# Moving the weight buffers of a split-precision kernel: high parts first, 128 spare bytes, then the raw slots

## The chip, the cores and the metric

One core of a Trainium2 chip runs the whole program. The time is the device time of one execution in microseconds. Weights come from the chip's memory through DMA queues; TensorE (PE, with its weight loads as PEld) multiplies, VectorE (DVE), ScalarE (ACT) and GpSimd (POOL) do the rest.

## What is computed

Two blocks in a row on 256 tokens of width 2048, all in float32. The first has two layers: an attention layer (two kinds of heads, 256 context tokens beside the 256 of the sequence, gates, a post-norm with modulation) and a Fourier layer (a two-dimensional FFT over tokens and channels in 16 groups, between two wide projections). The second has a mixer (a gated delta rule in both directions, and attention in three dilations) and a feed-forward part with a depthwise convolution. Most of the arithmetic lies in products of 256 activations with large weight matrices:

```python
z = h @ w_in                                               # attention, 2048 x 4928
u, gate = jnp.split(h @ w_in, 2, axis=-1)                  # Fourier, 2048 x 8192
proj = jnp.einsum("bsd,dp->bsp", n, w_in)                  # second mixer
up = depthwise_conv_centered(jnp.einsum("bsd,df->bsf", n, w_ffn_in), conv_ffn_w)
...
return jnp.einsum("bsf,fd->bsd", jax.nn.silu(gate) * val, w_ffn_out)
```

## The kernel before

**Units.** The host packs all weights into 479 units, in the order in which they are needed. A unit is up to 2048 floats per partition (8 KiB on each of 128 partitions): a few 128-row slices of a matrix by up to 768 columns. `UNITS` lists them; a `Linear` (`("ff", 3)`, `("oX", 1, 0)`, `"ckv"` and so on) is one product's share of them. 447 of the 479 are "split"; the others are `ada` units of the head, which are used as they land.

**Split precision.** A split unit goes through four hands. SP's queue loads it into a raw slot (L718). ACT copies it, rounded, into a high buffer as fp32r (L1459, in `act_hi`). DVE subtracts the high part from the raw weights and writes the remainder, the low part, back over the same raw slot (L2156, in `dve_lo`). PE then runs three matmuls for each slice and output tile (`pe_unit`; all matmuls are issued by the helper at L727): high weights by high activations, high weights by low activations, low weights by high activations. In most products the weights are the stationary operand and the 256 tokens move; in `fu`, `dv` and a few others the activations are stationary and the weights move.

**Buffers and their turns.** One tensor `slab` of 53,132 floats per partition holds all that lives in SBUF, and regions of it are laid out by hand. Region `W`, at offset 0, holds four raw slots and three high buffers of 2048 floats each (L518 to L520), and 32 floats (128 bytes) more, which nothing uses. Region `K` follows (constants, activations `X`), then `R` (everything that changes from stage to stage, such as the activations `H` and their high and low parts). In the head, the first 44 units, two more raw slots and one more high buffer exist inside `R`: by the code's sizes `high[3]` begins 4800 bytes past a multiple of 8192 bytes from the slab's start, `raw[4]` likewise, and `raw[5]` 7712 bytes past one. All seven buffers of `W` begin at exact multiples of 8192 bytes from the slab's start. `RAW_OF` and `HIGH_OF` give each unit its buffers by number: six and four in turn in the head, then four and three in turn.

**Order.** Each engine runs its own program and waits on semaphores. SP's DMA for a unit waits until PE has used the unit that held the raw slot before; ACT's copy waits for the landing and for the high buffer to come free; DVE's subtraction waits for ACT; PE waits for DVE. ACT and DVE run two units ahead of PE (`act_hi(LIN[name].us[n] + 2)`). The norms, softmaxes, the delta rule and the Fourier steps run as side work between units. In the delta rule four work areas, `gL`, `gY`, `gG[0]` and (through `gL`) `rhs[0]`, are laid over `high[0]`, `high[1]` and `high[2]` (L660 to L661), while no unit needs them.

The lines that matter: 

```python
W = Region(0, UNIT * (SLOTS + HIGH) + 32)                  # L518
raw = [W.place(UNIT) for _ in range(SLOTS)]
high = [W.place(UNIT) for _ in range(HIGH)]
K = Region(W.size, KEEP)
R = Region(W.size + KEEP, SLAB - KEEP - W.size)
```

Of the kernel before, what the change touches and what calls it, by code (L numbers as in the profile page):

```python
# [19 lines left out]
UNIT = 2048  # L20
SLOTS = 4
HIGH = 3
# [423 lines left out]
def program(nc, a, out, cmaps):  # L446
    with ExitStack() as ctx:
# [68 lines left out]
                return named  # L516

        W = Region(0, UNIT * (SLOTS + HIGH) + 32)  # L518
        raw = [W.place(UNIT) for _ in range(SLOTS)]
        high = [W.place(UNIT) for _ in range(HIGH)]  # L520
        K = Region(W.size, KEEP)
        R = Region(W.size + KEEP, SLAB - KEEP - W.size)

# [2620 lines left out]
```

## Time and profile before

| what | us |
|---|---|
| median of 3 runs | 2887.72 |
| lowest, highest | 2879.97, 2899.77 |
| the profiled execution | 2913.37 |
| span of the profiled execution, first to last instruction | 2911.6 |
| PE matmul busy | 2786.7 |
| DVE busy | 1809.9 |
| ACT busy | 1246.7 |

The profiled execution is longer than each of the three timed runs. The span is cut into stages by the order of the units: the head (0 to about 160 us), attention (to about 700), the Fourier layer (to about 1290), dilated attention (to about 1727), the delta rule (to about 2072), and from there the output product and the feed-forward part up to the end.

### The profile page before, as it was taken

What the parts mean: (1) busy time and instruction counts of PE and PEld (TensorE: products, weight loads), DVE (VectorE), ACT (ScalarE), POOL (GpSimd) and SP (SyncE); (2) the same over time, 40 slices, a digit from 0 to 9 for tenths busy, and PEclk for the clock granted to TensorE, in tenths of its full rate; (3) what the DMA queues carried; (4) which work ended last, traced back from release to release, by engine and by line L of the source; (5) the groups of instructions that cost most, each with busy time, mean ns of one, the idle gap of its engine ahead of it and who ended that gap; (6) DMA issues with size and microseconds to landing.
All of it is one profiled execution on the core that took longest, in us unless ns stands there. A gap on an engine that the chain in (4) does not pass through costs nothing.

```text
span 2911.6 us, 50366 instructions
## 1 busy us (share of the span) xinstructions
PE 2786.7 (96%) x22070; PEld 2638.8 (91%) x22070; DVE 1809.9 (62%) x2229; ACT 1246.7 (43%) x1375; POOL 270.2 (9%) x330
## 2 busy tenths in 40 slices
PE   6899999998999999989999999989999999999998
PEld 3598877797988998989999999979999999999998
DVE  2358767688777545566556555795666665466653
ACT  4323444345443334444434448453544443344444
POOL 0022002120111000003113110021000000000000
PEclk9899999998999999999999999999999999999999
DMA  9867535574776554435555544430445555555553
GB/s 368 325 226 247 194 133 201 202 277 149 251 247 225 192 199 162 169 136 190 174 173 175 174 167 146 154 139 1 145 160 188 189 181 188 189 184 187 183 185 138
DMA packets 93034, 546.84 MB, mean 188 GB/s; under 512 B 12656, under 2 KB 12816, under 8 KB 47888
## 3 DMA queue, kind: packets, MB, share of 16 engines
q1 hardware_dynamic: 69552, 466.39, 45.3%
q0 software_dynamic: 20480, 67.13, 6.8%
q10 hardware_dynamic: 2784, 10.11, 0.9%
q8 instruction: 174, 2.85, 0.4%
q14 instruction: 44, 0.36, 0.0%
HBM read 541.48 MB, written 2.10 MB: 187 GB/s over the span
## 4 chain that ended last, share of the span: by engine, by line
PE 67%; DVE 6%; ACT 2%; issue 2%; DMA 1%; DVEq 0%; ACTq 0%
PE bank L727 67%; DVE r L2156 2%; DVE f L2727 1%; ACT r L1459 1%; PE bank L787 1%; DVE f L2193 0%; DMA f<-in_later 0%; DVE f L2791 0%; ACT f L1821 0%; DVE f L2788 0%; DVE f L2804 0%; DVE f L2780 0%; DVE f L2539 0%; DMA f<-in_units 0%; DVE f L2556 0%
## 5 line engine op out<-in xcount | busy, mean ns | idle before, releaser
L727 PE MATMUL bank<-r,r 128*128 128x256 f32 (+1 forms) x19596 | 2444.1, 287 | 44.8 <-DVE r L2156 20.5
L727 PEld LDWEIGHTS bank<-r,r 128*128 128x128 f32 x19596 | 2376.2, 190 | 100.8 <-DVE r L2156 28.2
L2156 DVE TENSOR_TENSOR r<-f,r 128x2048 fp32r<-128x2048 f32 (+2 forms) x447 | 961.1, 2151 | 724.4 <-ACT r L1459 723.1
L1459 ACT CAST r<-f 128x2048 fp32r<-128x2048 f32 (+2 forms) x447 | 792.7, 1775 | 886.4 <-PE bank L727 684.2
L727 PE MATMUL bank<-f,f 128*128 128x128 f32 (+10 forms) x1992 | 326.5, 375 | 58.2 <-DMA f<-in_units 23.1
L727 PEld LDWEIGHTS bank<-f,f 128*128 128x128 f32 (+3 forms) x1992 | 218.8, 177 | 121.7 <-issue 53.1
L2193 DVE SCALAR_TENSOR_TENSOR f<-f,f,f 128x512 f32<-128x512 f32 x240 | 179.8, 749 | 53.8 <-DMA f<-in_later 38.2
L3052 POOL DMA_DIRECT2D f<-in_later x256 | 137.5, 537 | 799.8 <-DVE f L2193 475.8
L2727 DVE SCALAR_TENSOR_TENSOR f<-f,f,f 128x255 f32<-128x255 f32 (+1 forms) x272 | 132.9, 491 | 8.8
L1476 ACT COPY f<-bank 128x512 f32<-128x512 f32 x149 | 83.9, 584 | 115.6 <-PE bank L727 109.3
L3061 POOL TENSOR_TENSOR f<-f,f 32x512 f32<-32x512 f32 x24 | 62.7, 2614 | 658.4 <-DVE f L2665 658.4
L787 PEld LDWEIGHTS bank<-f,f 128*128 128x128 f32 x416 | 48.6, 146 | 41.5 <-issue 18.6
L787 PE MATMUL bank<-f,f 128*128 128x128 f32 x416 | 62.7, 284 | 13.7 <-ACT f L1642 9.2
L1642 ACT ACTIVATE f<-bank,f 128x512 f32<-128x512 f32 x32 | 22.0, 688 | 94.8 <-DVE f L2394 86.5
L3064 POOL TENSOR_TENSOR f<-f,f 32x512 f32<-32x512 f32 x24 | 43.7, 1820 | 1.9
L1776 ACT ACTIVATE f<-f,f 128x512 f32<-128x512 f32 x16 | 11.6, 724 | 75.1 <-DVE f L2684 75.1
L2392 DVE TENSOR_REDUCE f<-bank 128x1 f32<-128x512 f32 x32 | 22.0, 689 | 26.3 <-PE bank L727 26.3
L2199 DVE TENSOR_TENSOR f<-bank,f 128x8 f32<-128x8 f32 x8 | 1.3, 166 | 57.0 <-PE bank L727 57.0
L1592 ACT ACTIVATE f<-f 128x256 f32<-128x256 f32 (+1 forms) x46 | 17.3, 430 | 41.4 <-PE bank L727 41.3
L1752 ACT COPY f<-bank 128x254 f32<-128x254 f32 x16 | 5.9, 372 | 66.1 <-PE bank L727 66.1
L2718 DVE TENSOR_SCALAR f<-f,f 128x256 f32<-128x256 f32 x88 | 30.6, 347 | 0.0
L2416 DVE TENSOR_TENSOR f<-bank,f 128x512 f32<-128x512 f32 x24 | 16.6, 692 | 18.7 <-PE bank L727 17.7
(235 smaller groups left out, 925.2 us busy)
## 6 DMA issues: line engine op xcount, KB each, us to landing
f<-in_units SPq DMA_DIRECT2D x346, 1024.0 KB, 4.8
f<-in_units SPq DMA_DIRECT2D x124, 768.0 KB, 4.3
f<-in_later POOLq DMA_DIRECT2D x256, 256.0 KB, 4.3
f<-in_units SPq DMA_DIRECT2D x8, 576.0 KB, 4.4
f<-in_x ACTq DMA_DIRECT2D x2, 1024.0 KB, 12.8
f<-in_ctx ACTq DMA_DIRECT2D x2, 1024.0 KB, 12.2
f<-in_x_turned ACTq DMA_DIRECT2D x1, 2048.0 KB, 13.4
out<-f SPq DMA_DIRECT2D x4, 256.0 KB, 3.7
```

What stands on the lines that cost most here:

```text
L727: return e.matmul(o, lhsT, rhs, start=start, stop=stop, skip_group_check=True)
L787: ins = e.transpose(o[:, j * 128:(j + 1) * 128], src(j), ident)
L1459: e.copy(unit_view(high[HIGH_OF[u]][1], u), unit_view(raw[RAW_OF[u]][0], u)).then_inc(*up("w_hi", ("hi", u)))
L1476: return e.copy(dst, src(ps("lin", name, q))).then_inc(*up("act_out", ("out", "lin", name, q), *names))
L1642: e.activation(probs[i // 16][0][:, i % 3, :], ps("sc", i)[:, :], ACT.Exp, bias=mx[:, 1, i:i + 1], scale=scale, accum_out=mx[:, 2, i:i + 1 ...
L2156: e.tensor_tensor(unit_view(raw[RAW_OF[u]][1], u), unit_view(raw[RAW_OF[u]][0], u), unit_view(high[HIGH_OF[u]][1], u).bitcast(F32), ALU.su ...
L2193: ins = e.scalar_tensor_tensor(o, w, s, o, ALU.mult, ALU.add)
L2718: ins = e.tensor_scalar(o, s, tap(r), None, ALU.mult) if width == 3 else None
L2727: ins = e.scalar_tensor_tensor(o[:, lo:hi], s[:, lo + d:hi + d], tap(j), o[:, lo:hi], ALU.mult, ALU.add)
L3052: e.dma_start(own[:, m % 4, :], a["later"][m // 16, m // 2 % 8, :, m % 2 * 512:m % 2 * 512 + 512]).then_inc(*up(f"own_quarter{m % 4}", ("o ...
L3061: e.tensor_tensor(v, v, cos2.unsqueeze(1).to_broadcast([32, 2, T]), ALU.mult).then_inc(*up("pool_dil"))
L3064: e.tensor_tensor(v, v, two(rt[n % 2][0:32, :]), ALU.add).then_inc(*up("pool_dil", ("roped half", x, hf, br), ("half", n)))
```

## The change

Inside region `W` the three high buffers are placed first, then 32 floats are skipped, then the four raw slots are placed. The region's size is the same, so `K` and `R` and all in them stay where they were. In floats from the slab's start:

| buffer | before | after |
|---|---|---|
| high 0, 1, 2 | 8192, 10240, 12288 | 0, 2048, 4096 |
| raw 0, 1, 2, 3 | 0, 2048, 4096, 6144 | 6176, 8224, 10272, 12320 |
| spare 32 floats | 14336 | 6144 |

```diff
         W = Region(0, UNIT * (SLOTS + HIGH) + 32)
+        high = [W.place(UNIT) for _ in range(HIGH)]
+        W.at += 32
         raw = [W.place(UNIT) for _ in range(SLOTS)]
-        high = [W.place(UNIT) for _ in range(HIGH)]
```

## Rows read from the trace of the kernel before

**Rows 1.** The page: busy time, share of the span, instructions.
```profile
PE 2786.7 (96%) x22070; PEld 2638.8 (91%) x22070; DVE 1809.9 (62%) x2229; ACT 1246.7 (43%) x1375; POOL 270.2 (9%) x330
```
**Rows 2.** The page: the chain that ended last, by engine.
```profile
PE 67%; DVE 6%; ACT 2%; issue 2%; DMA 1%; DVEq 0%; ACTq 0%
```
**Rows 3.** Groups by line and form: busy us, mean ns, idle before and releasers.
```profile
L727 PE MATMUL bank<-r,r 128*128 128x256 f32 x18648 | 2230.9, 282 | 35.9 <-DVE r L2156 20.5 <-issue 8.0 <-DVE r L2592 5.0
L2156 DVE TENSOR_TENSOR r<-f,r 128x2048 fp32r<-128x2048 f32 x314 | 718.7, 2290 | 540.2 <-ACT r L1459 539.9
L1459 ACT CAST r<-f 128x2048 fp32r<-128x2048 f32 x314 | 599.6, 1911 | 672.5 <-PE bank L727 599.6 <-DMA f<-in_units 72.8
...
L1459 ACT CAST r<-f 128x1536 fp32r<-128x1536 f32 x124 | 183.4, 1481 | 210.0 <-DMA f<-in_units 127.9 <-PE bank L727 82.0
```
**Rows 4.** Stretches, L727 alone: from:to, length, PE busy (count), clock, DMA share, GB/s.
```profile
703.00:789.00 86.00, 86.00 (x732) 1.00 0.64 222
922.00:1074.00 152.00, 151.81 (x1339) 1.00 0.58 201
1466.00:1494.00 28.00, 28.00 (x233) 1.00 0.46 157
...
2520.00:2780.00 260.00, 260.00 (x2210) 1.00 0.53 186
```
**Rows 5.** L727 in the stretch 922 to 1074: durations, ns min/median/max.
```profile
L727 PE MATMUL bank<-r,r x1339: 275/276/364, 921.8 to 1073.9; 128*128 128x256 f32 x192
L727 PEld LDWEIGHTS bank<-r,r x1339: 187/188/192, 921.8 to 1073.9; 128*128 128x128 f32 x192
```
**Rows 6.** L727 in the stretch 2520 to 2780: durations, ns min/median/max.
```profile
L727 PE MATMUL bank<-r,r x2210: 280/281/282, 2519.8 to 2780.0; 128*128 128x256 f32 x185
L727 PEld LDWEIGHTS bank<-r,r x2209: 187/188/193, 2519.9 to 2780.0; 128*128 128x128 f32 x185
```
**Rows 7.** L727 on fp32r operands, five stretches from 250 to 2887 us: durations as before.
```profile
L727 PE MATMUL bank<-r,r x669: 273/276/684, 249.7 to 339.9; 128*128 128x256 f32 x166, 40*128 40x256 f32 x2
...
L727 PE MATMUL bank<-r,r x2063: 275/276/476, 891.7 to 1194.2; 128*128 128x256 f32 x153, 128*128 128x512 f32 x35
...
L727 PE MATMUL bank<-r,r x1155: 275/276/582, 1201.5 to 1354.9; 128*128 128x256 f32 x193
...
L727 PE MATMUL bank<-r,r x321: 275/276/369, 1424.8 to 1462.9; 128*128 128x256 f32 x161
...
L727 PE MATMUL bank<-r,r x6816: 280/281/550, 2072.4 to 2886.1; 128*128 128x256 f32 x195
```
**Rows 8.** L2156 and L1459 from 2100 to 2890 us, then 20 to 150; L2156 whole.
```profile
L2156 DVE TENSOR_TENSOR r<-f,r x141: 1751/2292/2294, 2102.9 to 2884.2; 128x2048 fp32r<-128x2048 f32 x125, 128x1536 fp32r<-128x1536 f32 x16
...
L1459 ACT CAST r<-f x141: 1457/1909/1916, 2101.0 to 2882.2; 128x2048 fp32r<-128x2048 f32 x125, 128x1536 fp32r<-128x1536 f32 x16
...
L2156 DVE TENSOR_TENSOR r<-f,r x12: 1748/1759/2293, 47.0 to 147.7; 128x1536 fp32r<-128x1536 f32 x8, 128x2048 fp32r<-128x2048 f32 x4
...
L1459 ACT CAST r<-f x13: 1457/1475/1913, 45.5 to 148.8; 128x1536 fp32r<-128x1536 f32 x8, 128x2048 fp32r<-128x2048 f32 x5
...
L2156 DVE TENSOR_TENSOR r<-f,r x447: 691/2291/2830, 47.0 to 2884.2; 128x2048 fp32r<-128x2048 f32 x100, 128x1536 fp32r<-128x1536 f32 x45, 128x1152 fp32r<-128x1152 f32 x4
```
**Rows 9.** ACT in order of time, 2200 to 2230: start us, us, instruction, idle before.
```profile
2205.58 1.91 ACT L1459 CAST r<-f 128x2048 fp32r<-128x2048 f32 x1 [3.22 <-PE bank L727]
2211.23 1.91 ACT L1459 CAST r<-f 128x2048 fp32r<-128x2048 f32 x1 [3.75 <-PE bank L727]
```
**Rows 10.** The DMA issues of L718, 2100 to 2890 us, then 20 to 150: microseconds to landing.
```profile
DMA to landing us min/median/max: 4.1/4.8/6.7
...
DMA to landing us min/median/max: 4.3/9.3/19.2
```
**Rows 11.** Waits, whole span: who waited for whom, us, times, longest.
```profile
PE bank L727 <- DMA f<-in_units: 23.1, 11, 4.7
PE bank L727 <- DVE r L2156: 20.5, 15, 5.2
```
**Rows 12.** The chain that ended last, shares by line, and its longest piece.
```profile
by line: PE bank L727 66.9%; issue 1.7%; DVE r L2156 1.5%; DVE f L2727 0.6%; ACT r L1459 0.6%; PE bank L787 0.5%; DVE f L2193 0.4%; DMA f<-in_later 0.4%; DVE f L2791 0.4%; ACT f L1821 0.4%; DVE f L2788 0.4%; DVE f L2804 0.3%; DVE f L2780 0.
...
2146.86 674.84 PE bank L727 x5712
```
**Rows 13.** Data rates by fortieths of 20 to 150 us, GB/s.
```profile
GB/s 433 413 426 418 426 413 422 412 429 426 161 330 376 436 421 35 40 406 417 417 432 424 290 3 300 378 418 429 406 13 26 374 426 418 432 351 425 179 408 266
```

## The prediction, as it was put on record

> **What bounds the kernel now.** I read the page's busy times first. PE multiplies for 96% of the span, DVE works for 62% and ACT for 43% [rows 1]. The chain that ended last lies with PE for 67% of its length, with DVE for 6% and with ACT for 2% [rows 2]. By line, the helper L727 alone holds 66.9%, the subtraction L2156 1.5% and the rounding copy L1459 0.6% [rows 12]. The longest piece of the chain is 5712 matmuls in 674.84 us without another engine between them, 118.1 ns from one to the next. So the time is the number of matmuls times the step from one to the next, and the change leaves the number alone.
>
> Next I asked what sets the step, since that is the one thing by which a change of addresses could reach the time. The matmul's own duration, 282 ns in the mean [rows 3], is longer than the step because matmuls overlap; the step has to be taken from stretches in which PE does nothing else. There are two values. From 922 to 1074 us 1339 matmuls fill 151.81 us, 113.4 ns each; from 2520 to 2780 us 2210 fill 260.00 us, 117.6 ns each [rows 4]. The shape is the same, the clock is at 1.00 (2.4 GHz) in both, and no matmul had to wait. The durations show the two steps once more: the median is 276 ns in the first stretch and 281 ns in the second, while the weight load has 188 ns in both [rows 5, 6]. The reader is to see that these are two conditions of the same instruction stream, each held for hundreds of matmuls with hardly any scatter (280, 281 and 282 ns are minimum, median and maximum of 2210).
>
> Is the slower one a matter of addresses? The stretch from 703 to 789 us takes 117.5 ns (86.00 over 732), and it holds units of the same product, the same activations and the same seven weight buffers as 922 to 1074 us (the `fg` products of the two Fourier halves) [rows 4]. Same operands at the same places, yet 4 ns apart. Within each stretch the buffers take turns, four raw and three high, so all twelve pairs come by, and the min/median/max of rows 6 leaves no room for a slot that costs more. The step is something that PE falls into and stays in; the address of a slot in multiples of 8192 bytes does not choose it.
>
> **The change, part by part.** Nothing is added or removed: the same DMAs, copies, subtractions and matmuls in the same order with the same waits. Two things move. The raw slots and the high buffers swap places in steps of whole slots, and the raw slots stand 128 bytes off the grid of 8192 bytes on which all seven stood before.
>
> *The swap of whole slots.* It changes the multiple of 8192 only. By the paragraph above the matmuls do not see it. For ACT and DVE, 125 full-size operations from 2100 to 2890 us run over all twelve pairs. The subtraction's median and maximum are 2292 and 2294 ns, the copy's 1909 and 1916 [rows 8]. Cost: 0 us.
>
> *The 128 bytes, DVE and ACT.* The head is a trial made by the kernel itself: its extra buffers lie 4800 and 7712 bytes off the grid, and its units mix them freely with buffers on the grid. The 12 subtractions there have 1748 to 2293 ns for both sizes, and the later 141 have 1751 to 2294; the copies 1457 to 1913 against 1457 to 1916 [rows 8]. An offset of another kind has no price there. Could the old placing, with every operand on one grid, have cost something that now goes away? A larger copy has 512 more elements for 1911 - 1481 = 430 ns [rows 3], 0.84 ns each, and the head's copies off the grid are not below that. Cost: 0 us. If they did become slower, the cover is wide in the last 800 us. There ACT starts a copy every 5.65 us and idles 3.2 to 3.8 us before it [rows 9]; copy and subtraction together are 1.91 + 2.29 = 4.2 us, and two units stand between a freed high buffer and its next need, 11.3 us. They could take twice as long and be hidden. Where there is no cover, in attention and the delta rule, the chain holds L2156 for 1.5% of 2911.6 us, 44 us. The dearest subtraction of the whole trace has 2830 ns against a median of 2291 [rows 8], 24% more for a reason that the rows don't give; were all of them so, 0.24 x 44 = 11 us would be added, and that is my upper end. Below nothing the bound is the 20.5 us that PE waits for L2156 in all [rows 11], which even a much quicker subtraction could at best remove.
>
> *The 128 bytes, DMA.* Late loads land in 4.8 us in the median and no more than 6.7 [rows 10], and nothing on PE waits for them between 2520 and 2780 us, where matmuls fill the stretch. In the head the loads do bind: 9.3 us to landing, and 23.1 us of waits by PE [rows 10, 11]. But there the slots off the grid were in use already, and the rate stood at 412 to 433 GB/s over the first ten fortieths [rows 13]. I take 0. The Trainium skill, "DMA: Bandwidth & Descriptors", section "How a descriptor splits into AXI transactions", says that a transfer which does not begin on a 256-byte boundary is given one transaction more; an 8192-byte row would go from 32 to 33, and if the head's 160 us were all bound by it the sum by that rule would be 160 / 32 = 5 us longer, an estimate from that page. Whether the slab itself begins on such a boundary no row shows, and by the code at least two of the head's three offsets (0, 4800 and 7712) are off one whichever way that is, and the rates just named are theirs too.
>
> *The 128 bytes, PE.* The low part's weight load (one in three) and the moving operand where weights move now begin 128 bytes off. The activations did not move. So this relation, between a load from `W` and a read from `R`, is new for a third of the matmuls. The near row for a less favourable read is 1466 to 1494 us, the `dv` products, where weights move and some stationary slices are read in steps of two: 28.00 over 233, 120.2 ns [rows 4]. Against 117.6 that is 2.6 ns; on a third of the 19,560 matmuls of split units, 6,520, it is 17 us. That is my upper end for a price on the low parts. The lower end is a gain: the same third at the fast step, 4.2 ns off, over those that are slow now. I take 0, because at every place where I looked matmuls have one of two medians, 276 and 281 ns, whatever buffers `R` and `W` lend them [rows 5 to 7]; the new offset would have to bring a third.
>
> The sum is 0 us on the profiled execution's 2913.37 us (span 2911.6). That execution was 25.6 us longer than the median of the timed runs, 2887.72, and longer than the highest of them. About the size of that difference is known: the 6816 matmuls from 2072 to 2887 us [rows 7] at 4.2 ns are 28.6 us, so one execution may have had its last stretch in the other condition. The forecast goes by the median: 2888 us.
>
> **The rivals.** *The last stretch falls into the fast step.* Something small (a wait that ends a few ns sooner beside a new address) decides which condition PE is in when it leaves the side work near 2072 us, and it then keeps it for 6816 matmuls. Worth 28.6 us there, and with the 732 of 703 to 789 us another 3: 2888 - 32 = 2856. For it: the two conditions exist, nothing in the code names them, and the last stretch, at 281 ns, is long [rows 7]. Against it: the trigger would have to be an address, and the `fg` products show both at the same addresses; and the timed runs may have had it already.
>
> *The fast stretches fall into the slow step.* The same mechanism with the sign turned: 669 + 2063 + 1155 matmuls, and three times the 321 of a stretch that comes back in the dilated stage [rows 7], 4,850 in all with a median of 276 ns, at 4.2 ns: +20 us, 2908. It stays within 1%.
>
> *The low parts' loads cost more.* This is the rival that ends on the slower side. Its place is each third matmul of a split unit, where the weights are read 128 bytes off. The price by the row of the `dv` products is 17 us, 2905. It decides for "slower by over 1%" from 28.9 / 6520 = 4.4 ns for each low-part matmul, just over the difference between the two steps; if one such load throws the whole stream to the dearer step, all 19,560 pay 2.6 ns, 51 us, 2939. Against it is that the durations of loads in rows 5 and 6 are alike to 1 ns over four raw and three high buffers and every column offset within them.
>
> *A shared grid cost something before, and now does not.* Gain through all of PE: bounded by the fast step everywhere, which is 28.6 + 3 plus a few us for the slow parts of the first 700 us and the delta rule; about 2845. Against it: full-size operations show no scatter, as they would if collisions came and went.
>
> **How the numbers follow.** No effect that the engines see: 0.62. The last stretch turns fast: 0.12 (2856). The grid's cost goes away: 0.05 (2845). The fast stretches turn slow: 0.07 (2908), of which 0.03 together with dearer subtractions, which brings it past 2917. Low parts dearer: 0.14, of which 0.03 at 2905 and 0.11 from 2917 to 2939. The likeliest has its own range, 2880 to 2900, which is that of the runs shown. The range for 8 in 10 reaches to 2855 below and 2918 above: it leaves out the grid's 0.05 and nearly all of the 0.14 above 2917, together just under 2 in 10. One per cent, about what a measurement of this kernel can tell from no change, is 28.9 us: faster means under 2859, slower over 2917. Faster: 0.12 + 0.05 = 0.17. Slower: 0.03 + 0.11 = 0.14. Same: the rest, 0.69.
>
> **What would show each step right or wrong.** Right: in the changed kernel's profile the subtraction stays at 2292 ns, the copy at 1909, late landings at 4.8 us, the weight load at 188, and the matmul's median is 276 or 281 ns in each long stretch. The difference in span should then be, within a few us, the number of matmuls that changed condition times 4.2 ns. Wrong: a third median; a load or subtraction whose duration differs between early and late by more than 10 ns; waits of PE for L2156 or for the loads that grew by over 10 us; or a step of 113.4 ns in every stretch, which would say that addresses choose the condition after all.

## The result, and the profile after

The changed kernel takes 2876.5 us in the median of 20 executions against 2889.23 for the kernel before in as many; the ratio is 0.9946, with a 95% interval of 0.9926 to 0.9967 (it is not the quotient of the two medians, which is 0.9956). Each ratio of this document leaves out executions more than 1.5% above the fastest of their own kernel: here one of 7048.27 us, and further down two, of 2931.43 and 2938.75 us, of the kernel with the gap in the middle. The gain is half a per cent, within 1%, but not "no effect": the interval excludes 1, the medians are 12.7 us apart, and the mechanisms that I had in that direction had chances of only 0.12 and 0.05. The profiled execution took 2881.78 us, with a span of 2880.0.

Busy times of the changed kernel, then its chain by line (all lines after L518 have moved by one, L727 is now L728):

```profile
PE 2746.8 (95%) x22070; PEld 2596.6 (90%) x22070; DVE 1808.7 (63%) x2229; ACT 1248.2 (43%) x1375; POOL 271.6 (9%) x330
```
```profile
by line: PE bank L728 65.3%; issue 1.9%; DVE r L2157 1.7%; ACT r L1460 0.7%; DVE f L2728 0.6%; PE bank L788 0.5%; DVE f L2792 0.4%; ACT f L1822 0.4%; DVE f L2789 0.4%; DVE f L2805 0.3%; DVE f L2194 0.3%; DVE f L2540 0.3%; DVE f L2781 0.3%; 
...
2142.96 650.57 PE bank L728 x5712
```

Against [rows 1] PE is busy for 40 us less, and DVE and ACT within 2 us of before. The longest piece of the chain has the same 5712 matmuls as in [rows 12] and takes 650.57 us instead of 674.84: 24.3 of the 31.6 us by which the two spans differ. So the step from one matmul to the next has changed. L728 in the stretches of [rows 4], then durations in ns (min/median/max) from 922 to 1074 us, from 2520 to 2780 and from 2072 to 2887:

```profile
703.00:789.00 86.00, 85.14 (x736) 0.99 0.61 214
922.00:1074.00 152.00, 151.00 (x1314) 0.99 0.56 199
1466.00:1494.00 28.00, 28.00 (x233) 1.00 0.49 169
...
2520.00:2780.00 260.00, 260.00 (x2297) 1.00 0.54 191
```
```profile
L728 PE MATMUL bank<-r,r x1314: 275/276/415, 922.8 to 1073.9; 128*128 128x256 f32 x188
...
L728 PE MATMUL bank<-r,r x2297: 276/276/277, 2519.8 to 2780.0; 128*128 128x256 f32 x192
...
L728 PE MATMUL bank<-r,r x6904: 276/276/552, 2071.8 to 2867.6; 128*128 128x256 f32 x198
```

In the late stretch 2297 matmuls fit where 2210 did: 260 / 2297 = 113.2 ns instead of 117.6. (A window also counts the matmuls that began just before it and reach into it, so each step taken this way reads about 0.1 ns low, alike in all kernels.) The median of 281 ns of [rows 6, 7] is gone; 276 ns stands in each stretch of [rows 5 to 7]. The `dv` products from 1466 to 1494 us are nearly as slow as before, 233 matmuls in 28 us. The subtractions, copies and loads, which the prediction had costed at nothing, did cost nothing. The subtraction and the copy from 2100 to 2870 us, and the loads there and from 20 to 150 us:

```profile
L2157 DVE TENSOR_TENSOR r<-f,r x141: 1751/2292/2294, 2100.2 to 2853.1; 128x2048 fp32r<-128x2048 f32 x125, 128x1536 fp32r<-128x1536 f32 x16
...
L1460 ACT CAST r<-f x141: 1475/1909/1917, 2098.3 to 2851.2; 128x2048 fp32r<-128x2048 f32 x125, 128x1536 fp32r<-128x1536 f32 x16
...
DMA to landing us min/median/max: 4.0/4.8/7.3
...
DMA to landing us min/median/max: 4.3/8.7/18.9
```

The medians are those of [rows 8, 10] for DVE, ACT and the late loads; the early loads have 8.7 us where they had 9.3.

**Entering and leaving the slow step.** Both kernels have side work near their end (a few narrow matmuls), after which PE starts on the last unit. First the changed kernel, the first microsecond after the side work and the four after it; then the kernel before at the same unit:

```profile
L728 PE MATMUL bank<-r,r x8: 277/280/364, 2862.1 to 2863.0; 128*128 128x256 f32 x8
...
L728 PE MATMUL bank<-r,r x41: 276/276/283, 2862.9 to 2867.5; 128*128 128x256 f32 x41
```
```profile
L727 PE MATMUL bank<-r,r x9: 278/281/364, 2893.4 to 2894.4; 128*128 128x256 f32 x9
...
L727 PE MATMUL bank<-r,r x38: 281/281/282, 2894.4 to 2898.8; 128*128 128x256 f32 x38
```

Both leave the side work in the slow step, at 280 and 281 ns. The changed kernel drops out of it after eight or nine matmuls; the kernel before stays in it to the end of the unit. So the change did not stop PE from falling into the slow step here. It took away its hold.

### The profile page after: what moved, and what is told of

Its sections match the earlier page's. It is cut to its first block, busy times and chain, and to the rows that moved or that the text cites. A ratio compares the mean times of both kernels' runs of the same rounds, so it can differ in the third digit from the quotient of the medians.

```text
span 2880.0 us, 50366 instructions
## 1 busy us (share of the span) xinstructions
PE 2746.8 (95%) x22070; PEld 2596.6 (90%) x22070; DVE 1808.7 (63%) x2229; ACT 1248.2 (43%) x1375; POOL 271.6 (9%) x330
## 4 chain that ended last, share of the span: by engine, by line
PE 66%; DVE 7%; ACT 2%; issue 2%; DVEq 0%; ACTq 0%
PE bank L728 65%; DVE r L2157 2%; ACT r L1460 1%; DVE f L2728 1%; PE bank L788 1%; DVE f L2792 0%; ACT f L1822 0%; DVE f L2789 0%; DVE f L2805 0%; DVE f L2194 0%; DVE f L2540 0%; DVE f L2781 0%; DVE f L2557 0%; ACT L1810 0%; DVE r L2563 0%
## 5 line engine op out<-in xcount | busy, mean ns | idle before, releaser
L728 PE MATMUL bank<-r,r 128*128 128x256 f32 (+1 forms) x19596 | 2404.5, 285 | 53.8 <-DVE r L2157 26.6
L728 PEld LDWEIGHTS bank<-r,r 128*128 128x128 f32 x19596 | 2335.3, 190 | 112.2 <-DVE r L2157 30.6
L728 PE MATMUL bank<-f,f 128*128 128x128 f32 (+10 forms) x1992 | 327.2, 377 | 58.0 <-DMA f<-in_units 22.3
L728 PEld LDWEIGHTS bank<-f,f 128*128 128x128 f32 (+3 forms) x1992 | 218.6, 176 | 121.6 <-issue 52.7
L2423 DVE SCALAR_TENSOR_TENSOR f<-bank,f,f 128x256 f32<-128x256 f32 x48 | 21.0, 479 | 12.2 <-PE bank L728 11.4
## 6 DMA issues: line engine op xcount, KB each, us to landing
f<-in_x ACTq DMA_DIRECT2D x2, 1024.0 KB, 12.7
```

The source lines that it names most:

```text
L728: return e.matmul(o, lhsT, rhs, start=start, stop=stop, skip_group_check=True)
```

## The experiments

The question is which relation of addresses does this. The expectations name five theories. A: the distance between high and low parts counts. B: the place of the raw slots (the low parts) against the activations counts; in its wider form, that of the high parts too, each by itself. C: the order of the whole slots counts. D: each execution falls into one step or the other by chance. P: the relation repeats after 256 bytes.

The activations `H` and their parts begin, by the code's sizes, 94,912 bytes into the slab, 192 past a multiple of 256, and what the late stretch reads of weights and activations follows at multiples of 256 from these starts. In the table, "high" and "low" are the starts of the high buffers and the raw slots (which hold the low parts) less that of the activations, in bytes modulo 256; the step is 260 us over the number of matmuls from 2520 to 2780 us of each profile. Two values stand where profiles of one kernel differ. The ratio is to the kernel before on the same chip.

| kernel | high / low | step, ns | ratio (95%) |
|---|---|---|---|
| before_again (step also from three other profiles of before) | 64 / 64 | 117.6 or 113.2 | 0.9996 (0.996 to 1.003) |
| swap_only | 64 / 64 | 117.6 | 1.0005 (0.997 to 1.004) |
| raw_minus_256 | 64 / 64 | 117.6 | 0.9995 (0.995 to 1.004) |
| the change | 64 / 192 | 113.2 | 0.9946 (0.993 to 0.997) |
| raw_minus_128 | 64 / 192 | 113.2 | 0.9933 (0.990 to 0.996) |
| gap_in_middle | 192 / 64 | 113.2 or 118.8 | 1.0078 (1.003 to 1.012) |
| gap_first | 192 / 192 | 117.6 | 1.0144 (1.010 to 1.019) |
| no_spare | 192 / 192 | 117.6 | 1.0133 (1.009 to 1.018) |
| gap_64_bytes | 64 / 128 | 118.1 | 1.0164 (1.012 to 1.021) |
| gap_32_bytes | 64 / 96 | 118.7 | 1.0190 (1.014 to 1.024) |
| both_plus_64 | 128 / 128 | 118.5 | 1.0181 (1.011 to 1.025) |
| high_minus_64_raw_plus_64 | 0 / 128 | 119.0 | 1.0186 (1.013 to 1.024) |
| both_minus_64 | 0 / 0 | 119.9 | 1.0226 (1.017 to 1.028) |

One step, 117.6 ns, stands beside ratios of 1.00 and of 1.014, because the last stretch is not the whole time. At 64 / 64 that stretch is fast in two of four profiles of before, and the piece of 1712 matmuls in the second Fourier half takes 238.38 us in three of them. At 192 / 192 the last stretch is slow in both profiles, and that piece takes 245.19 us in both.

**Before again.** No edit.

> The kernel before, unchanged, with a profile of another execution. If each execution falls into the slow or the fast step by chance (theory D), this profile should show another pattern of stretches than the first, perhaps with the last stretch of 6,800 matmuls at a median of 276 ns, and a span down to 2880 us. If addresses alone hold the slow step (A, B or C), long stretches at 281 ns are still there, in whichever places, and 276 ns does not fill the whole profile. Ratio 1.00 by each.

Span 2905.9 us, ratio 1.00, and 281 ns from 2520 to 2780 us once more. Theory D is not settled by it: the `fg` products of the first Fourier half are fast in it, but the last stretch is slow both times. The `fg` products are a second case of both steps at the same addresses and in the same place of the program. The executions say more: of the 29 of the kernel before in this comparison 19 took 2877 to 2893 us and 10 took 2908 to 2916, with nothing in between.

**The order alone.**

```diff
+        high = [W.place(UNIT) for _ in range(HIGH)]
         raw = [W.place(UNIT) for _ in range(SLOTS)]
-        high = [W.place(UNIT) for _ in range(HIGH)]
```

> High buffers first, raw slots right behind them, the spare 32 floats at the end: the order is changed and every buffer stays on the grid of 8192 bytes. Theory C (the order of whole slots matters): as the changed kernel, 276 ns nearly everywhere, ratio 0.995. Theories A and B (the 128 bytes matter): long stretches at 281 ns as before, ratio 1.00.

1.0005 (0.997 to 1.004), with the same slow last stretch. Theory C falls. The order of the buffers, the visible part of the change, has no effect that can be told from none.

**The gap between them, order of before.**

```diff
         raw = [W.place(UNIT) for _ in range(SLOTS)]
+        W.at += 32
         high = [W.place(UNIT) for _ in range(HIGH)]
```

> Raw slots first as before, then the 32 spare floats, then the high buffers: low and high parts are 128 bytes apart on the grid, and the raw slots stand to the activations as they did; the high buffers are moved against them. Theory A (high against low parts): 276 ns nearly everywhere, ratio 0.995. Theory B (raw slots against activations): long stretches at 281 ns, ratio 1.00.

1.0078, slower; neither theory had that. By the medians of all executions it is 2926.02 us against 2886.31, 1.4% slower: eight of the 12 took 2925 to 2939 us and four 2887 to 2901. Low and high parts are 128 bytes apart as in the change, so theory A in its plain form falls.

**The gap ahead of all seven.**

```diff
+        W.at += 32
         raw = [W.place(UNIT) for _ in range(SLOTS)]
         high = [W.place(UNIT) for _ in range(HIGH)]
```

> The 32 spare floats first, then raw slots and high buffers as before: all seven are moved by 128 bytes against the activations, and low and high parts share one grid. Theory A: long stretches at 281 ns, ratio 1.00. Theory B: 276 ns nearly everywhere, ratio 0.995. If neither this nor the kernel with the gap in the middle turns fast, the order and the gap would be needed together.

1.0144. The sign is against both theories as I had put them (1.00 and 0.995). But it shows that the weights' place against the rest matters with no difference at all between high and low parts, which leads to the next one.

**The rest moved instead of the weights.**

```diff
-        W = Region(0, UNIT * (SLOTS + HIGH) + 32)
+        W = Region(0, UNIT * (SLOTS + HIGH))
```

> The 32 spare floats are left out and the order is that of before. The weights keep their places, and the constants, the activations and all else behind them move down by 128 bytes. Against the activations all seven buffers then stand as in the kernel with the gap first. If the relation of weights to activations decides (theory B, which the gap-first kernel's 1.014 speaks for): median 279 to 281 ns in nearly all stretches and ratio 1.014. If the place in the slab itself decides: as before, both steps in long stretches, ratio 1.00.

1.0133, and the durations of the late stretch are those of the kernel with the gap first (that one, then this one, 2520 to 2780 us):

```profile
L728 PE MATMUL bank<-r,r x2210: 279/279/280, 2519.7 to 2779.9; 128*128 128x256 f32 x185
L728 PEld LDWEIGHTS bank<-r,r x2209: 187/188/188, 2519.8 to 2779.9; 128*128 128x128 f32 x185
```
```profile
L727 PE MATMUL bank<-r,r x2210: 279/279/280, 2519.8 to 2779.9; 128*128 128x256 f32 x185
L727 PEld LDWEIGHTS bank<-r,r x2209: 187/188/188, 2519.9 to 2779.9; 128*128 128x128 f32 x185
```

Same counts, same three numbers, although in one the weights moved and in the other everything else. What counts is the difference of the addresses, not the addresses. And 279 ns is a duration that the kernel before never had as a median of a long stretch: placing does choose which steps there are.

**Other distances.** The changed kernel with `W.at += 16` and `W.at += 8` in place of 32:

> As the changed kernel with 64 bytes between high and raw instead of 128. If any small distance between the low parts' loads and the grid ends the slow step: 276 ns nearly everywhere, ratio 0.995. If the distance has to be 128 bytes: another mix, long stretches at 281 ns, ratio 1.00 or more.

> As the changed kernel with 32 bytes between high and raw. Any small distance is enough: ratio 0.995 and 276 ns. A distance of 32 bytes is nothing to the memory: as the kernel with the swap alone, ratio 1.00 and long stretches of both steps.

1.0164 and 1.0190: both are dearer than no gap at all, and for 32 bytes neither theory had that. The step is no longer one number either; in the second it runs over 281 to 286 ns:

```profile
L728 PE MATMUL bank<-r,r x2190: 281/282/286, 2519.7 to 2780.0; 128*128 128x256 f32 x200
```

**The mirror, and twice the distance.** The order of before with a gap of 32, or 64, floats in the middle and a region larger by as many beyond, so that the high buffers keep their relation to the activations and the raw slots go down by 128, or 256, bytes (the slab grows by 32 or 64 floats):

```diff
-        W = Region(0, UNIT * (SLOTS + HIGH) + 32)
+        W = Region(0, UNIT * (SLOTS + HIGH) + 64)
         raw = [W.place(UNIT) for _ in range(SLOTS)]
+        W.at += 32
         high = [W.place(UNIT) for _ in range(HIGH)]
```

> Raw slots first, 32 floats, high buffers, and a region larger by 32 floats, so that everything behind it moves up by 128 bytes: against the activations the high buffers stand as before and the raw slots 128 bytes lower, the mirror of the change. If what counts is that low parts are off the high parts' grid while these keep their old relation to the activations: 276 ns nearly everywhere, ratio 0.995. If the sign counts: long stretches at 279 to 281 ns or a mix as in the kernel with the gap in the middle, ratio 1.00 to 1.01.

> Against the activations the high buffers stand as before and the raw slots 256 bytes lower. Moves of +128 and -128 gave the same (0.995 and 0.993), moves of 32 and 64 bytes 1.019 and 1.016. If the relation of addresses repeats every 256 bytes (theory P), this is the kernel before: long stretches of both steps, ratio 1.00. If what helps is distance between low and high parts (theory A), more of it helps as much: 276 ns nearly everywhere, ratio 0.994.

Down by 128 bytes is as good as up by 128, and down by 256 is the kernel before, slow last stretch included. The first of the next two is raw_minus_128, the second raw_minus_256:

```profile
L728 PE MATMUL bank<-r,r x2296: 276/276/276, 2519.8 to 2779.9; 128*128 128x256 f32 x192
```
```profile
L728 PE MATMUL bank<-r,r x2210: 281/281/281, 2519.7 to 2779.9; 128*128 128x256 f32 x185
```

The relation repeats after 256 bytes. Theory P holds as far as these two distances go.

**Against the activations by 64.** The region `R` moved up by 16 floats with all weights on one grid; the same with the change's gap; and all weights up by 16 floats:

```diff
-        R = Region(W.size + KEEP, SLAB - KEEP - W.size)
+        R = Region(W.size + KEEP + 16, SLAB - KEEP - W.size - 16)
```

> All seven buffers on one grid, high buffers first; the stages' region is moved up by 64 bytes, so that weights stand 64 bytes lower against the activations and both begin on one 256-byte grid. If the worst place for a weight load is the activations' own (both reads hit the same part of the memory at once), the ratio is above 1.014, that of the move by 128. If the grid shared by all is good, 276 ns nearly everywhere and 0.994.

> As the changed kernel (128 bytes between high and raw), but with the stages' region moved up by 64 bytes: high parts 64 bytes lower and low parts 64 bytes higher against the activations than before. If the 128 bytes between high and low parts are what counts, whatever the activations do (theory A): 276 ns nearly everywhere, ratio 0.995. If each of the two relations to the activations counts by itself (theory B in its wider form): another step, ratio above 1.00, since the moves by 64 bytes have been dear so far.

> All seven buffers on one grid, moved up by 64 bytes against the activations. By theory B in its wider form this is dear, 1.01 to 1.02, as the low parts alone at 64 bytes were (1.016). If high and low parts on one grid behave alike at every distance from the activations, 1.00 to 1.014.

All three are slow, and the worst of all is the one in which weights and activations begin on the same 256-byte grid, with 119.9 ns and no scatter. It is also the only one in which the weight load's duration moves, from 188 ns to 192:

```profile
L727 PE MATMUL bank<-r,r x2169: 283/283/283, 2519.8 to 2780.0; 128*128 128x256 f32 x198
L727 PEld LDWEIGHTS bank<-r,r x2169: 192/192/192, 2519.8 to 2780.0; 128*128 128x128 f32 x198
```

The second has the change's 128 bytes between high and low parts and is 1.9% slower than the kernel before. The gap between them is not what helps; both relations to the activations count, as the wider theory B has it.

**Four more profiles**, to see what the two groups of executions are:

> The kernel before once more, for a trace of another execution. Its timed executions lie in two groups, about 2885 and about 2911 us, 26 us apart, and both traces so far are from the upper group with 281 ns in the last stretch. If that stretch is the difference: an execution of the lower group shows a median of 276 ns there and a span near 2884; one of the upper group repeats 281 ns.

> As the look before it. If the two groups have another cause than the last stretch, a trace of the lower group has 281 ns there and is shorter elsewhere.

> The kernel with the gap in the middle had groups at about 2892 and 2928 us, and its trace is from the lower one, with the last stretch at 276 ns up to its last part. A trace from the upper group should show a slow last stretch, above 281 ns in the median or 118 ns from one matmul to the next.

> The changed kernel once more. If its addresses let PE leave the slow step wherever it enters it, the second trace repeats the first: 276 ns as the median of every long stretch and a span of 2869 to 2880 us. If the first trace was lucky (theory D), some stretch is at 281 ns.

The two executions of before took 2887.31 and 2895.01 us, and both have 276 ns in the last stretch, at the addresses that had 281 twice. The second is longer mainly because the Fourier stage is slow in it: its piece of 1712 matmuls takes 243.09 us against 238.38. The one with the gap in the middle took 2935.74 us against 2900.54 for its first profile; its last stretch has a median of 280 ns, but the expected longer step, 118.8 ns. The late stretch of before's third profile (before_look_2), then the longest piece of the chain in it, in the gap-in-middle kernel's two profiles, and in the changed kernel's second:

```profile
L727 PE MATMUL bank<-r,r x2296: 276/276/276, 2519.8 to 2779.9; 128*128 128x256 f32 x192
```

```profile
2147.56 649.95 PE bank L727 x5712
```
```profile
2159.61 649.16 PE bank L728 x5712
```
```profile
2163.81 681.75 PE bank L728 x5712
```
```profile
2137.72 649.95 PE bank L728 x5712
```

Four times the same 5712 matmuls. The kernel before does them in 649.95 or in 674.84 us [rows 12] (its other two profiles have 650.16 and 675.03), and these 25 us are about the distance between its groups. The changed kernel had the fast one in both its profiles, as expected for the second, and 19 of its 20 timed executions lie between 2870 and 2882 us. So theory D holds for the kernel before, whose step is not fixed by its addresses, and not for the changed one.

**Where the rest of the gain lies.** Before's third profile, from its lower group, and the changed kernel's second differ by 11.4 us in span (2885.5 and 2874.1) with the same last piece. Pieces of the two chains, before first:

```profile
1312.87 113.81 PE bank L727 x954
1466.13 70.37 PE bank L727 x582
1575.95 70.37 PE bank L727 x582
1685.77 51.04 PE bank L727 x420
2074.77 60.11 PE bank L727 x528
```
```profile
1311.18 110.90 PE bank L728 x954
1461.59 69.21 PE bank L728 x582
1570.32 69.21 PE bank L728 x582
1679.05 50.58 PE bank L728 x420
2065.97 60.13 PE bank L728 x528
```

The starts drift apart: 1.7 us at 1312, 6.7 us at 1686, 8.8 us at 2075, 9.8 us at the last piece. The first 1.7 us are within what profiles of before differ by there (1310.42 to 1319.58 us). What follows is not: from the piece at 1312 to the last one the four profiles of before take 832.4 to 835.3 us, the changed kernel's two 827.5 and 826.5. The dilated stage gives 5.0 us of it and the delta rule 2.1. In the dilated stage two stretches of some hundred matmuls come back three times, slow before and fast now. One of them, then one stretch each of the delta rule and of the `dv` products, the last from the first profiles of both kernels; of each pair before comes first:

```profile
L727 PE MATMUL bank<-r,r x107: 281/281/283, 1399.4 to 1411.9; 128*128 128x256 f32 x107
L728 PE MATMUL bank<-r,r x107: 275/276/282, 1395.7 to 1407.7; 128*128 128x256 f32 x107
...
L727 PE MATMUL bank<-r,r x308: 281/281/281, 1859.8 to 1896.0; 128*128 128x256 f32 x154
L728 PE MATMUL bank<-r,r x279: 275/276/386, 1851.8 to 1884.0; 128*128 128x256 f32 x140
...
L727 PE MATMUL bank<-r,r x143: 279/282/290, 1469.3 to 1486.4; 128*128 128x256 f32 x143
L728 PE MATMUL bank<-r,r x145: 280/282/287, 1470.3 to 1487.4; 128*128 128x256 f32 x145
```

The `dv` products, in which the weights move, keep their 282 ns.

## Why the prediction was wrong

**Right.** PE's step from matmul to matmul is what the time is made of, and at the placing of before it has two values that PE holds for hundreds of matmuls. The swap of whole slots is free (swap_only, 1.0005). The durations of DVE, ACT and the loads do not show the 128 bytes. Of raw slots 0, 32, 64 and 128 bytes past one grid, at most one kind can lie on a 256-byte boundary, and PE's waits for loads do not tell them apart: 23.1 us before [rows 11], 22.3 with the change, and with 32 bytes between high and raw

```profile
PE bank L728 <- DMA f<-in_units: 22.5, 10, 3.2
```

The rule of the Trainium skill, "DMA: Bandwidth & Descriptors", section "How a descriptor splits into AXI transactions", that the prediction weighed is thus borne out by no run here; the 5 us estimated from it do not appear in these waits. And the surmise was right that the profiled execution of before had its last stretch in the slow step while many of the timed ones had not.

**Wrong, first step.** "The address of a slot in multiples of 8192 bytes does not choose it" was true, and I read it as "addresses do not choose it". The `fg` products in both steps at the same addresses show only that placing does not fix the step. They leave open that it decides how firmly PE is held in one. The comparison could not show more: the seven buffers stood on one grid, so they had a single relation modulo 256, 64 / 64. The head's three extra buffers had others, but not the change's either: by the code's sizes they stand 0, 0 and 96 bytes from the activations modulo 256, not 192.

**Wrong, second step.** This is the step that failed. Of the 128 bytes on PE it says "I take 0", because everywhere matmuls have one of two medians "whatever buffers `R` and `W` lend them". The runs showed a gain of 12.7 us in the median, and in the chains it lies in this term: between the two profiled executions PE is busy for 40 us less, and the late stretch has 113.2 ns for each matmul where it had 117.6. The trial in the head was too thin for a zero. A few units use the off-grid buffers, among side work, and after the restart shown above the changed kernel, too, spends eight matmuls at 280 ns. A median over a mixed stretch cannot see it. I had even written that the new offset "would have to bring a third"; it did not have to, it only had to let go of one. Other offsets do bring a third: 279, 282 and 283 ns. Of the signs that the prediction lists, one of its last came almost in full: the fast step in every long stretch but the `dv` products, "which would say that addresses choose the condition after all".

**Wrong, the rivals' sizes.** Two rivals had a part of it. "The last stretch falls into the fast step" (0.12, 2856) had the right place and a wrong sum: it took the 28.6 us off the median, though the stretch was already fast in two of four profiles and, to judge by the times, in 19 of 29 executions. What the median gains is the slow stretches elsewhere, about 11 us by the two profiles compared, and the end of the upper group. "A shared grid cost something before" (0.05) had the right cause. Its evidence against, that operations show no scatter, does not hold: the step at 0 / 0 is the dearest of all and has 283 ns as minimum, median and maximum. A steady cost has no scatter.

The Trainium skill, "SBUF — State Buffer", section "Who interferes with whom", lists PE's two ways of reading, for the moving operand and for weight loads, as independent of one another. The steps of 113.2 to 119.9 ns, which follow the difference of the two operands' addresses modulo 256, disagree with that, if it is read as a rule on time.

**What stays open.** Why the step depends on that difference. That a weight load and the moving operand, read at the same time, meet in some part of the memory would fit the worst case at 0 / 0, where both have their longest median durations, but no run shows the parts. Other engines also read and write both regions meanwhile, and no run moves the weights against PE's moving operand alone; 2169 matmuls of exactly 283 ns, while ACT and DVE work in turns, speak against them. What picks the step at 64 / 64, where four profiles of one kernel enter the last stretch twice fast and twice slow, is open too. Nor is it shown which matmul of the three is held up at 64 / 64, or why the slow step holds there and not at 64 / 192.

## What to carry to other kernels

Where PE is the bound and its matmuls follow one another closely, take the step from a long clean stretch (busy time over count) of several profiles, not one. Two values of it at the same shape, clock and addresses mean that PE can be held in a slow condition, and then the difference between the addresses of weights and activations, modulo 256 bytes, is worth a trial in steps of 32 to 128 bytes: here kernels that differ in the placing alone ran from 0.993 to 1.023 of the kernel before. A row in which all buffers share one relation says nothing of another relation; "no scatter" excludes a cost that comes and goes, not one that is always there.

## What the runs showed of the hardware

A stream of matmuls of 128x128 weights by 256 moving activation columns in fp32r, at the granted clock of 1.00 (2.4 GHz), has a step of 113.2, 117.6, 118.1, 118.5, 118.7, 118.8, 119.0 or 119.9 ns, by the placement of weights against activations modulo 256 bytes. At one placement (64 / 64) two of these exist side by side, and one piece of 5712 matmuls took 649.95 us or 674.84. At another (64 / 192) the slower was left after eight or nine matmuls where it was looked at. The durations tell the steps apart only in part. The matmul's median goes from 276 to 283 ns, but 117.6 ns stands with 281 at 64 / 64 and with 279 at 192 / 192. The weight load's is 188 ns in all but one, and 192 at 0 / 0.
